# Two transformer blocks on one core: attention with its probabilities turned three steps after their scores in place of two

## The chip, the cores and the metric

The kernel runs on one core of a Trainium2 chip. The metric is the device time of one execution in microseconds (us), lower is better. Engines are named as in the profile: PE is TensorE's matmuls, PEld its weight loads, DVE is VectorE, ACT is ScalarE, POOL is GpSimd, SP is SyncE with the DMA queue.

## The reference, cut to what matters

Two blocks of two layers each work on 512 tokens of width 1024 in float32. Three of the four layers begin with an attention of 16 heads of 64, and these are what the change touches: a sparse one ("a" in the kernel), one with a forget gate ("b") and one with grouped keys over all tokens ("c"). All three have this core, for blocks of 128 queries:

```python
def one_block(q_blk):
    s = jnp.einsum('bqkgd,bskd->bkgqs', q_blk, k).astype(jnp.float32) * scale
    p = jax.nn.softmax(s, axis=-1).astype(v.dtype)
    return jnp.einsum('bkgqs,bskd->bqkgd', p, v)
```

In "a" a mask of selected keys is added to the logits, in "b" a decay and a causal mask. A block of queries i (0 to 3) in "a" and "b" needs only the first (i + 1) x 128 keys; in "c" it needs all 512. The rest of the model, projections and MLPs, is matmul work that the change leaves alone.

## The kernel before, in words

Every engine has its own program, in order, tied to the others by semaphores. Nothing is planned by a scheduler: the order is written out by hand, and each engine waits where its program says `wait_ge`.

One attention is `attend`, once in each of the programs of TensorE, ScalarE and VectorE. It goes through 32 steps (`STEPS`): 8 pairs of heads c, and for each the 4 query blocks i. A step has two rows (r = 2n and 2n + 1), one for each head of the pair. The life of step n:

- TensorE, `scores(n)`: two score matmuls (L525) into two of four banks; in "b" two more with the decay (L533). They wait until VectorE has emptied these banks of step n - 2.
- VectorE (L1254 in "a" and "b", L1252 in "c"): scales or masks the scores into the row's buffer `PROBS[a][r % 6]` (tiles PA, PBB, PC) and takes their extreme value. It waits until the buffer's old row has been turned.
- ScalarE (L917): the exponential in place, with its sum.
- VectorE (L1267, L1269), one iteration later: reciprocal of the sum, and the probabilities scaled by it.
- TensorE, `turn(n)` (L547), two iterations after the scores: transposes of 128x128 blocks into bank 4 (first row of the step) and bank 5 (second row). It waits for the scaled probabilities (`pn_done`) and for the copies that emptied these banks of step n - 1.
- The turned rows are copied into `TURNED` (tiles TA, TB, TC, six buffers each): the first row of the even steps by VectorE (L1261), all others by ScalarE (L926).
- TensorE, `values(n)` (L560), three iterations after the scores: the sums with the values into bank 6 or 7, by pair of heads.
- When the four steps of a pair are done, ScalarE copies its bank to `Xhi` (L930), and VectorE then takes the rest into `Xlo` (L1273). Both are at the ends of their iteration's part: iterations 7, 11, 15 and so on.

In an iteration n TensorE does scores(n), turn(n - 2), values(n - 3). VectorE does the scores of n, in even iterations the copy of step n - 2, the probabilities of step n - 1, and at 7, 11, ... the Xlo. ScalarE does the exponentials of n, its copies of step n - 2, and at 7, 11, ... the Xhi. In "a" VectorE also finishes the selection of keys (L1373, L1375) within its first three iterations. GpSimd makes the masks MH for "b" (L1691), one per pair of heads. The attention is followed by its output projection (L415 to L417), which reads Xhi and Xlo.

Of the kernel before, what the change touches and what calls it, by code (L numbers as in the profile page):

```python
# [9 lines left out]
F32 = mybir.dt.float32  # L10
F32R = mybir.dt.float32r

P = 128
# [5 lines left out]
EPS = 1e-6  # L19
BIG = 1e30  # L20
# [88 lines left out]
def body(nc, ctx, t, consts, out):  # L109
# [25 lines left out]
    stat = sb("stats", [P, 6, 4])  # L135
# [30 lines left out]
    with ExitStack() as region:  # L166
        QA = sb("QA", [P, KC, S], F32, region)
        KA = [sb(f"KA{i}", [P, S], F32, region) for i in range(4)]
        VA = sb("VA", [P, NT, 256], F32, region)
        PA = [sb(f"PA{i}", [P, S], F32, region) for i in range(6)]  # L170
        TA = [sb(f"TA{i}", [P, S], F32, region) for i in range(6)]
        QI, KI, WI = sb("QI", [P, 4, S], F32, region), sb("KI", [P, S], F32, region), sb("WI", [P, NT, 8], F32, region)
        SC = [sb(f"SC{i}", [P, S], F32, region) for i in range(3)]
        SC2, top = sb("SCW", [P, S], F32, region), sb("top", [P, 8], F32, region)
        RL = [sb(f"RL{i}", [P, S], F32, region) for i in range(3)]
        M = [sb(f"MA{i}", [P, (i + 1) * P], F32, region) for i in range(NT)]
        rope_a = sb("rope_a", [P, 2, S], F32, region)
# [6 lines left out]
    with ExitStack() as region:  # L184
        QB, KB, VB = sb("QB", [P, KC, S], F32, region), sb("KB", [P, KC, S], F32, region), sb("VB", [P, NT, D], F32, region)
        PBB = [sb(f"PBB{i}", [P, S], F32, region) for i in range(6)]
        TB = [sb(f"TB{i}", [P, S], F32, region) for i in range(6)]
        LF, FT = sb("LF", [P, 4, NT * 16], F32, region), sb("FT", [16, S], F32, region)
        CK, CQ = sb("CK", [P, S], F32, region), sb("CQ", [P, S], F32, region)
        MH = [sb(f"MH{i}", [P, S], F32, region) for i in range(2)]  # L190
        tsum, tri = sb("tsum", [P, S], F32, region), sb("tri", [P, S], F32, region)
    with ExitStack() as region:
        QC = sb("QC", [P, KC, S], F32, region)
        KCC = [sb(f"KC{i}", [P, S], F32, region) for i in range(4)]
        VC = sb("VC", [P, NT, 256], F32, region)
        PC = [sb(f"PC{i}", [P, S], F32, region) for i in range(6)]
# [166 lines left out]
    def tensor_program(pe):  # L363
# [151 lines left out]
        def attend(a, heads_q, heads_k, heads_v):  # L515
# [20 lines left out]
            def turn(n):  # L536
                for e in range(2):
                    r = 2 * n + e
                    pe_until.wait_ge(pn_done, base + r + 1)
                    if r >= 2:  # L540
                        by_act, by_dve = turned_by(a, r - 2)
                        if (r - 2) % 4:
                            pe_until.wait_ge(tr_act, by_act)
                        else:
                            pe_until.wait_ge(tr_dve, by_dve)
                    for j in range(0, width(a, STEPS[n][1]), P):
                        m = pe.transpose(bank[4 + e][:, j:j + P], PROBS[a][r % 6][:, j:j + P], ident[:])  # L547
                    m.then_inc(tr_full, 1)
# [281 lines left out]
    def scalar_program(act):  # L830
# [78 lines left out]
        def attend(a):  # L909
            base = 64 * ATT[a]  # L910
            for n in range(len(STEPS) + 4):
                if n < len(STEPS):
                    w = width(a, STEPS[n][1])
                    for r in (2 * n, 2 * n + 1):
                        p, st = PROBS[a][r % 6], stat[:, r % 6, :]
                        act_until.wait_ge(sc_out, base + r + 1)
                        act.activation(p[:, 0:w], p[:, 0:w], ACT_F.Exp, bias=st[:, 0:1], scale=-1.0, accum_out=st[:, 1:2]).then_inc(ex_done, 1)  # L917
                if 2 <= n < len(STEPS) + 2:
                    w = width(a, STEPS[n - 2][1])
                    for e in range(2):  # L920
                        r = 2 * (n - 2) + e
# [219 lines left out]
    def vector_program(dve):  # L1141
# [93 lines left out]
        def attend(a, mask, before=None):  # L1235
            base, hi0 = 64 * ATT[a], fill_base(a + "o")[0]
            for n in range(len(STEPS) + 4):
                if n < len(STEPS):
# [4 lines left out]
                    for r in (2 * n, 2 * n + 1):  # L1243
                        p, st = PROBS[a][r % 6], stat[:, r % 6, :]
# [10 lines left out]
                if 2 <= n < len(STEPS) + 2 and (2 * (n - 2)) % 4 == 0:  # L1255
                    r = 2 * (n - 2)
                    w = width(a, STEPS[n - 2][1])
# [4 lines left out]
                if 1 <= n < len(STEPS) + 1:  # L1262
                    w = width(a, STEPS[n - 1][1])
                    for r in (2 * n - 2, 2 * n - 1):
                        p, st = PROBS[a][r % 6], stat[:, r % 6, :]
# [4 lines left out]
                if n >= 4 and (n - 4) % NT == NT - 1:  # L1270
                    c = (n - 4) // NT
# [566 lines left out]
```

## Time and profile before

| | us |
|---|---|
| median of 3 runs | 2792.96 (2792.11 to 2793.75) |
| the profiled execution | 2792.17 |
| its span in the profile | 2790.6 |
| attention "a", first scores to the projection's first matmul | 110.61 |
| attention "b", the same | 99.95 |
| attention "c", the same | 111.55 |

Over the whole span PE is busy 2677.3 us (96%), its weight loads 2124.1, DVE 1331.2, ACT 968.6, POOL 1063.6. The three attentions lie at 155, 838 and 1456 us. In the timeline an entry begins with its start and its length in us; "x4" says how many instructions are merged into it; what stands in brackets is how long the engine had been idle before, and who released it. The first row of a step and the second have two instructions each in the scores, as a float32 matmul is recorded as two.

### The profile page before, as it was taken

What the parts mean: (1) busy time and instruction counts of PE and PEld (TensorE: products, weight loads), DVE (VectorE), ACT (ScalarE), POOL (GpSimd) and SP (SyncE); (2) the same over time, 40 slices, a digit from 0 to 9 for tenths busy, and PEclk for the clock granted to TensorE, in tenths of its full rate; (3) what the DMA queues carried; (4) which work ended last, traced back from release to release, by engine and by line L of the source; (5) the groups of instructions that cost most, each with busy time, mean ns of one, the idle gap of its engine ahead of it and who ended that gap; (6) DMA issues with size and microseconds to landing.
All of it is one profiled execution on the core that took longest, in us unless ns stands there. A gap on an engine that the chain in (4) does not pass through costs nothing.

```text
span 2790.6 us, 32354 instructions
## 1 busy us (share of the span) xinstructions
PE 2677.3 (96%) x13002; PEld 2124.1 (76%) x13002; DVE 1331.2 (48%) x2341; ACT 968.6 (35%) x1587; POOL 1063.6 (38%) x474
## 2 busy tenths in 40 slices
PE   8968999999998999999999999999999999999999
PEld 6645788887775678888775778888787888788887
DVE  4786598862016478883458542221325233332221
ACT  4345332222336432322437443322323232342231
POOL 4510444443451244444340234444444334344442
PEclk9979999999999999999999999999999999999999
DMA  4100455542220155553210123223332222233322
GB/s 138 61 16 16 128 186 183 186 139 76 92 91 1 46 160 191 183 184 98 83 61 1 46 77 105 91 92 104 123 105 69 91 91 77 76 105 97 99 91 76
DMA packets 259432, 274.42 MB, mean 98 GB/s; under 512 B 6868, under 2 KB 249300, under 8 KB 259028
## 3 DMA queue, kind: packets, MB, share of 16 engines
q1 hardware_dynamic: 259284, 272.37, 30.4%
q8 instruction: 103, 1.69, 0.3%
q14 instruction: 45, 0.37, 0.0%
HBM read 270.25 MB, written 2.10 MB: 98 GB/s over the span
## 4 chain that ended last, share of the span: by engine, by line
PE 90%; DVE 6%; ACT 3%; issue 1%; DMA 0%; POOL 0%; SPq 0%; DVEq 0%; ACTq 0%
PE bank L415 23%; PE bank L417 23%; PE bank L416 23%; PE bank L547 2%; PE bank L464 2%; PE bank L466 2%; PE bank L465 2%; PE bank L560 2%; PE bank L393 2%; PE bank L525 2%; PE bank L394 2%; PE bank L395 2%; DVE top L1373 1%; PE bank L795 1%; PE bank L513 1%
## 5 line engine op out<-in xcount | busy, mean ns | idle before, releaser
L1625 POOL TENSOR_TENSOR wlo<-raw,whi 128x1024 fp32r<-128x1024 f32 (+1 forms) x408 | 986.0, 2438 | 1504.2 <-ACT whi L844 1504.1
L415 PE MATMUL bank<-Xhi,whi 128*128 128x512 f32 (+1 forms) x1616 | 642.7, 398 | 7.0 <-POOL wlo L1625 6.9
L417 PE MATMUL bank<-Xhi,wlo 128*128 128x512 f32 (+1 forms) x1616 | 631.2, 391 | 0.0
L416 PE MATMUL bank<-Xlo,whi 128*128 128x512 f32 (+1 forms) x1616 | 630.7, 390 | 0.0
L844 ACT ACTIVATE whi<-raw 128x1024 fp32r<-128x1024 f32 (+1 forms) x408 | 404.9, 1041 | 591.3 <-PE bank L417 514.5
L415 PE MATMUL bank<-Hhi,whi 128*128 128x512 f32 x1024 | 406.7, 397 | 0.0
L416 PE MATMUL bank<-Hlo,whi 128*128 128x512 f32 x1024 | 404.9, 395 | 0.0
L417 PE MATMUL bank<-Hhi,wlo 128*128 128x512 f32 x1024 | 404.9, 395 | 0.0
L415 PEld LDWEIGHTS bank<-Xhi,whi 128*128 128x128 f32 (+1 forms) x1616 | 303.5, 188 | 78.3 <-issue 15.3
L416 PEld LDWEIGHTS bank<-Xlo,whi 128*128 128x128 f32 (+1 forms) x1616 | 303.6, 188 | 66.2 <-issue 3.6
L417 PEld LDWEIGHTS bank<-Xhi,wlo 128*128 128x128 f32 (+1 forms) x1616 | 303.2, 188 | 65.5
L1286 DVE SCALAR_TENSOR_TENSOR acc<-ada,cond,acc 128x256 f32<-128x256 f32 x336 | 345.8, 1029 | 12.0
L1190 DVE SCALAR_TENSOR_TENSOR HT<-bank,MOD,HT 128x512 f32<-128x512 f32 x96 | 72.0, 751 | 420.3 <-PE bank L417 401.3
L1319 DVE TENSOR_TENSOR tmp<-tmp 128x512 f32<-128x512 f32 x128 | 111.4, 871 | 258.0 <-ACT tmp L942 257.9
L417 PEld LDWEIGHTS bank<-Hhi,wlo 128*128 128x128 f32 x1024 | 192.4, 188 | 46.5
L416 PEld LDWEIGHTS bank<-Hlo,whi 128*128 128x128 f32 x1024 | 192.5, 188 | 45.5
L415 PEld LDWEIGHTS bank<-Hhi,whi 128*128 128x128 f32 x1024 | 192.4, 188 | 45.4
L942 ACT ACTIVATE tmp<-bank 128x512 f32<-128x512 f32 x128 | 76.5, 598 | 423.3 <-PE bank L417 408.4
L1188 DVE TENSOR_TENSOR HT<-bank,HT 128x512 f32<-128x512 f32 x80 | 55.1, 688 | 196.1 <-PE bank L417 196.1
L464 PE MATMUL bank<-whi,Xhi 128*128 128x512 f32 x256 | 101.9, 398 | 2.5 <-DVE Xlo L1167 2.5
L466 PE MATMUL bank<-whi,Xlo 128*128 128x512 f32 x256 | 100.4, 392 | 0.0
L465 PE MATMUL bank<-wlo,Xhi 128*128 128x512 f32 x256 | 100.4, 392 | 0.0
(257 smaller groups left out, 3000.1 us busy)
## 6 DMA issues: line engine op xcount, KB each, us to landing
ada<-in_ada_w SPq DMA_DIRECT2D x48, 1024.0 KB, 6.1
raw<-in_w_up SPq DMA_DIRECT2D x32, 1024.0 KB, 5.6
raw<-in_w_down SPq DMA_DIRECT2D x32, 1024.0 KB, 5.1
raw<-in_mlp_w_in SPq DMA_DIRECT2D x32, 1024.0 KB, 5.5
raw<-in_mlp_w_out SPq DMA_DIRECT2D x32, 1024.0 KB, 5.0
raw<-in_gmlp_w_in SPq DMA_DIRECT2D x24, 1024.0 KB, 5.1
raw<-in_gmlp_w_out SPq DMA_DIRECT2D x12, 1024.0 KB, 5.0
raw<-in_w_in_a SPq DMA_DIRECT2D x8, 1024.0 KB, 5.5
```

The source lines that it names most:

```text
L415: pe.matmul(b[0:rows, :], whi[s][:, c, j:j + rows], hi[:, c, :], start=(c == 0), stop=False)
L416: pe.matmul(b[0:rows, :], whi[s][:, c, j:j + rows], lo[:, c, :], start=False, stop=False)
L417: m = pe.matmul(b[0:rows, :], wlo[s][:, c, j:j + rows], hi[:, c, :], start=False, stop=(c == KC - 1))
L464: pe.matmul(b[:], Xhi[:, c, q * P:(q + 1) * P], hi[:, k, :], start=(c == 0), stop=False)
L465: pe.matmul(b[:], Xhi[:, c, q * P:(q + 1) * P], lo[:, k, :], start=False, stop=False)
L466: m = pe.matmul(b[:], Xlo[:, c, q * P:(q + 1) * P], hi[:, k, :], start=False, stop=(c == KC - 1))
L844: act.activation(whi[u % 2][:, c0:c1, 0:k], src[:, c0:c1, 0:k], ACT_F.Copy).then_inc(hi_done, 1)
L942: act.activation(tmp[v % 2][:], bank[(gm.tile + o) % 4][:], ACT_F.Relu).then_inc(up_q, 1)
L1190: dve.scalar_tensor_tensor(HT[:, o, :], b[:], gate[:, o:o + 1], HT[:, o, :], ALU.mult, ALU.add).then_inc(h_set, 1)
L1286: dve.scalar_tensor_tensor(a[:], src[:, c, :], cd[:, c:c + 1], a[:], ALU.mult, ALU.add).then_inc(ada_step, 1)
L1319: dve.tensor_tensor(r[:], tmp[v % 2][:], tmp[v % 2][:], ALU.mult).then_inc(up_r, 1)
L1625: pool.tensor_tensor(wlo[u % 2][:, c0:c1, 0:k], src[:, c0:c1, 0:k], whi[u % 2][:, c0:c1, 0:k].bitcast(F32), ALU.subtract).then_inc(lo_done, 1)
```

## The change

The distances and the number of row buffers get names. Rows are kept in 8 buffers in place of 6, with 8 places for their sums and extremes; the turn of a step follows its scores at three iterations in place of two, and its values at five in place of three. TensorE's order in an iteration becomes scores(n), turn(n - 3), values(n - 5). ScalarE and VectorE follow with their copies, and Xhi and Xlo come at iterations 9, 13, ... in place of 7, 11, ... The six buffers of turned rows stay, and so does who copies which row.

```diff
+ROWS, TURN, SUM = 8, 3, 5
...
-    stat = sb("stats", [P, 6, 4])
+    stat = sb("stats", [P, ROWS, 4])
...
-        PA = [sb(f"PA{i}", [P, S], F32, region) for i in range(6)]
+        PA = [sb(f"PA{i}", [P, S], F32, region) for i in range(ROWS)]
...
-                        m = pe.transpose(bank[4 + e][:, j:j + P], PROBS[a][r % 6][:, j:j + P], ident[:])
+                        m = pe.transpose(bank[4 + e][:, j:j + P], PROBS[a][r % ROWS][:, j:j + P], ident[:])
...
-            for n in range(len(STEPS) + 3):
+            for n in range(len(STEPS) + SUM):
                 if n < len(STEPS):
                     scores(n)
-                if 2 <= n < len(STEPS) + 2:
-                    turn(n - 2)
-                if n >= 3:
-                    values(n - 3)
+                if TURN <= n < len(STEPS) + TURN:
+                    turn(n - TURN)
+                if n >= SUM:
+                    values(n - SUM)
...
-                if n >= 4 and (n - 4) % NT == NT - 1:
-                    c = (n - 4) // NT
-                    act_until.wait_ge(pv_done, 32 * ATT[a] + n - 3)
+                if n > SUM and (n - SUM) % NT == 0:
+                    c = (n - SUM) // NT - 1
+                    act_until.wait_ge(pv_done, 32 * ATT[a] + n - SUM)
                     act.activation(Xhi[:, c, :], bank[6 + c % 2][:], ACT_F.Copy).then_inc(x_hi, 1)
...
-                        if r >= 6:
-                            dve_until.wait_ge(tr_full, base + r - 5)
+                        if r >= ROWS:
+                            dve_until.wait_ge(tr_full, base + r - ROWS + 1)
...
-                if 2 <= n < len(STEPS) + 2 and (2 * (n - 2)) % 4 == 0:
-                    r = 2 * (n - 2)
-                    w = width(a, STEPS[n - 2][1])
+                if TURN <= n < len(STEPS) + TURN and (n - TURN) % 2 == 0:
+                    r = 2 * (n - TURN)
+                    w = width(a, STEPS[n - TURN][1])
```

## Rows read from the trace of the kernel before

**Rows 1.** Busy time in the three attentions: PE, PEld, DVE, ACT, POOL; clock; DMA
```profile
155.06:265.67 110.61, 79.55 (x609) 49.02 (x609) 84.40 (x316) 58.41 (x183) 0.00 (x0) 0.84 0.01 1
838.13:938.08 99.95, 87.31 (x737) 54.74 (x737) 67.67 (x279) 59.56 (x184) 9.38 (x6) 1.00 0.00 1
1456.33:1567.88 111.55, 102.54 (x896) 64.48 (x897) 94.54 (x279) 76.52 (x184) 0.00 (x0) 1.00 0.01 1
```
**Rows 2.** By line: what L547 and L1273 waited for (us in all, times)
```profile
  DVE PC L1269: 42.2, 50
  DVE PA L1269: 42.0, 41
...
  ACT Xhi L930: 33.0, 24
```
**Rows 3.** Timeline of PE in "c": a period, and steps without a stall
```profile
1497.72 1.25 PE L547 MATMUL bank<-ident,PC 128*128 128x128 f32 x8 [0.89 <-DVE PC L1269]
...
1505.25 1.09 PE L560 MATMUL bank<-TC,VC 128*64 128x128 f32 x16
1506.28 1.13 PE L525 MATMUL bank<-KC,QC 64*128 64x512 f32 x4
...
1509.38 1.13 PE L525 MATMUL bank<-KC,QC 64*128 64x512 f32 x4
1511.40 1.25 PE L547 MATMUL bank<-ident,PC 128*128 128x128 f32 x8 [0.89 <-DVE PC L1269]
```
**Rows 4.** Timeline of VectorE and ScalarE in "c", around one Xlo
```profile
1502.43 0.69 DVE L1261 COPY TC<-bank 128x512 f32<-128x512 f32 x1
...
1504.33 0.75 DVE L1252 TENSOR_SCALAR_CACHE_REDUCE PC<-bank,RQ 128x512 f32<-128x512 f32 x1
...
1506.55 1.06 ACT L926 ACTIVATE TC<-bank 128x512 f32<-128x512 f32 x2
...
1507.50 0.59 ACT L930 ACTIVATE Xhi<-bank 128x512 fp32r<-128x512 f32 x1
1508.12 0.69 DVE L1273 TENSOR_TENSOR Xlo<-bank,Xhi 128x512 fp32r<-128x512 f32 x1 [1.18 <-ACT Xhi L930]
...
1508.73 0.74 DVE L1252 TENSOR_SCALAR_CACHE_REDUCE PC<-bank,RQ 128x512 f32<-128x512 f32 x1
```
**Rows 5.** Timeline of "a": PE's stalled turns, VectorE and ScalarE between them
```profile
202.82 0.84 PE L547 MATMUL bank<-ident,PA 128*128 128x128 f32 x6 [1.32 <-ACT TA L926]
...
206.14 0.42 DVE L1254 CUSTOM_DVE_ANT_0 PA<-bank,MA 128x256 f32<-128x256 f32 x1
...
207.60 1.06 ACT L926 ACTIVATE TA<-bank 128x512 f32<-128x512 f32 x2
...
208.62 0.56 DVE L1254 CUSTOM_DVE_ANT_0 PA<-bank,MA 128x384 f32<-128x384 f32 x1 [0.92 <-PE bank L525]
...
210.44 0.25 ACT L926 ACTIVATE TA<-bank 128x128 f32<-128x128 f32 x1
...
213.89 0.84 PE L547 MATMUL bank<-ident,PA 128*128 128x128 f32 x6 [1.32 <-ACT TA L926]
...
214.53 0.69 DVE L1273 TENSOR_TENSOR Xlo<-bank,Xhi 128x512 fp32r<-128x512 f32 x1 [0.94 <-ACT Xhi L930]
...
215.55 0.55 DVE L1261 COPY TA<-bank 128x384 f32<-128x384 f32 x1
```
**Rows 6.** Timeline of PE in "b": two stalled turns, a period apart
```profile
858.11 0.84 PE L547 MATMUL bank<-ident,PBB 128*128 128x128 f32 x6 [1.09 <-ACT TB L926]
...
870.53 0.85 PE L547 MATMUL bank<-ident,PBB 128*128 128x128 f32 x6 [1.09 <-ACT TB L926]
```
**Rows 7.** The ends of "a" and "b" on PE, and a stretch's busy time with its clock
```profile
262.48 3.26 PE L560 MATMUL bank<-TA,VA 128*64 128x128 f32 x28
...
936.30 1.85 PE L560 MATMUL bank<-TB,VB 128*64 128x128 f32 x28
...
262.00:264.00 2.00, 2.00 (x17) 1.67 (x17) 0.00 (x0) 0.93 (x2) 0.00 (x0) 0.50 0.00 0
```

More of the change, by code:

```diff
@@ L185, in body @@
         QB, KB, VB = sb("QB", [P, KC, S], F32, region), sb("KB", [P, KC, S], F32, region), sb("VB", [P, NT, D], F32, region)
-        PBB = [sb(f"PBB{i}", [P, S], F32, region) for i in range(6)]
+        PBB = [sb(f"PBB{i}", [P, S], F32, region) for i in range(ROWS)]
         TB = [sb(f"TB{i}", [P, S], F32, region) for i in range(6)]
@@ L195, in body @@
         VC = sb("VC", [P, NT, 256], F32, region)
-        PC = [sb(f"PC{i}", [P, S], F32, region) for i in range(6)]
+        PC = [sb(f"PC{i}", [P, S], F32, region) for i in range(ROWS)]
         TC = [sb(f"TC{i}", [P, S], F32, region) for i in range(6)]
@@ L910, in attend @@
             base = 64 * ATT[a]
-            for n in range(len(STEPS) + 4):
+            for n in range(len(STEPS) + SUM + 1):
                 if n < len(STEPS):
@@ L914, in attend @@
                     for r in (2 * n, 2 * n + 1):
-                        p, st = PROBS[a][r % 6], stat[:, r % 6, :]
+                        p, st = PROBS[a][r % ROWS], stat[:, r % ROWS, :]
                         act_until.wait_ge(sc_out, base + r + 1)
                         act.activation(p[:, 0:w], p[:, 0:w], ACT_F.Exp, bias=st[:, 0:1], scale=-1.0, accum_out=st[:, 1:2]).then_inc(ex_done, 1)
-                if 2 <= n < len(STEPS) + 2:
-                    w = width(a, STEPS[n - 2][1])
+                if TURN <= n < len(STEPS) + TURN:
+                    w = width(a, STEPS[n - TURN][1])
                     for e in range(2):
-                        r = 2 * (n - 2) + e
+                        r = 2 * (n - TURN) + e
                         if r % 4:
@@ L1236, in attend @@
             base, hi0 = 64 * ATT[a], fill_base(a + "o")[0]
-            for n in range(len(STEPS) + 4):
+            for n in range(len(STEPS) + SUM + 1):
                 if n < len(STEPS):
@@ L1243, in attend @@
                     for r in (2 * n, 2 * n + 1):
-                        p, st = PROBS[a][r % 6], stat[:, r % 6, :]
+                        p, st = PROBS[a][r % ROWS], stat[:, r % ROWS, :]
                         b = bank[2 * (n % 2) + r % 2]
                         dve_until.wait_ge(sc_full, base + r + 1)
-                        if r >= 6:
-                            dve_until.wait_ge(tr_full, base + r - 5)
+                        if r >= ROWS:
+                            dve_until.wait_ge(tr_full, base + r - ROWS + 1)
                         mk = mask(i, w)
@@ L1254, in attend @@
                             dve.tensor_tensor_reduce(p[:, 0:w], b[:, 0:w], mk, -0.125, 3e38, ALU.add, ALU.min, st[:, 0:1]).then_inc(sc_out, 1)
-                if 2 <= n < len(STEPS) + 2 and (2 * (n - 2)) % 4 == 0:
-                    r = 2 * (n - 2)
-                    w = width(a, STEPS[n - 2][1])
+                if TURN <= n < len(STEPS) + TURN and (n - TURN) % 2 == 0:
+                    r = 2 * (n - TURN)
+                    w = width(a, STEPS[n - TURN][1])
                     dve_until.wait_ge(tr_full, base + r + 1)
@@ L1264, in attend @@
                     for r in (2 * n - 2, 2 * n - 1):
-                        p, st = PROBS[a][r % 6], stat[:, r % 6, :]
+                        p, st = PROBS[a][r % ROWS], stat[:, r % ROWS, :]
                         dve_until.wait_ge(ex_done, base + r + 1)
@@ L1269, in attend @@
                         dve.tensor_scalar(p[:, 0:w], p[:, 0:w], st[:, 2:3], None, ALU.mult).then_inc(pn_done, 1)
-                if n >= 4 and (n - 4) % NT == NT - 1:
-                    c = (n - 4) // NT
+                if n > SUM and (n - SUM) % NT == 0:
+                    c = (n - SUM) // NT - 1
                     dve_until.wait_ge(x_hi, hi0 + c + 1)
```

## The prediction

> **What bounds the kernel now.** I read the three attentions first as stretches, since the change touches nothing else. They last 110.61, 99.95 and 111.55 us, together 322.1 of a span of 2790.6 us, and in none of them is an engine full: PE records 79.55, 87.31 and 102.54 us, DVE 84.40, 67.67 and 94.54, ACT less [rows 1]. Then I read who is waited for. The transposes (L547) have waits of 42.0 us on the scaled probabilities (L1269) in "a" and 42.2 in "c", PE's and the weight loads' own records counted together; and VectorE sat idle for 33.0 us ahead of its 24 instructions on L1273, waiting for ScalarE's Xhi (L930) [rows 2]. The first wait is what the change names. The second lies in VectorE's queue, ahead of the next step's scores (L1252, L1254).
>
> Last I read single steps. In "c" a step without a stall takes PE 3.10 us (1506.28 to 1509.38), a period of four 13.68 (from one stalled turn at 1497.72 to the next at 1511.40), so 13.68 - 4 x 3.11 = 1.25 us of every period are idle [rows 3]. They come from one place. In every fourth iteration, which I call the flush, VectorE ends its probabilities at 1506.94, waits 1.18 us for Xhi, runs L1273 (0.61 us to the next issue) and takes the next scores at 1508.73 [rows 4]; those were ready about 1507.4, and all that follows is late. The period of "a" is 11.07 us (202.82 to 213.89); PE's first stall in it is 1.32 us, on ScalarE's pair of copies (L926), and the rest is on L1269 [rows 5]. That of "b" is 12.42, with 1.09 on ScalarE's copies [rows 6].
>
> **PE without stalls.** By the steps that don't wait, scores take PE 1.06 us at 512 columns and 0.21 less per 128 columns, a transposed pair 0.37, 0.58, 0.78 or 1.02 us by width, the values 0.37, 0.58, 0.81 or 1.03 (1505.25 to 1506.28) [rows 3]. Summed over the widths 128 to 512: "a" 8.5 us a period, "b" about 10.7 (its masks add matmuls), "c" 12.43. VectorE's own sums with L1273 are 8.5 in "a" and "b" and 12.4 in "c". So there are 2.5, 1.7 and 1.25 us a period to win, and in "a" and "c" PE and VectorE would then be tied.
>
> **The change, part by part.**
> (1) Turning at three steps. The wait on L1269 goes: it is ready a whole iteration ahead. Next late is the copy out of the transposes' bank, since the transposes of iteration n wait for the copies of iteration n-1, which stand on ScalarE behind that iteration's two exponentials. This tie does not get looser by the change.
> (2) The parity. VectorE copies the even steps' first row (L1261). With distance 2 that fell in even iterations, with distance 3 in odd ones; the flush, with values at five in place of three, falls at 9, 13, ... in place of 7, 11, ..., odd both times. So VectorE's copy now lies in the flush iteration, where ScalarE has one copy ahead of Xhi in place of two. In "c", counted from VectorE's start of the scores: ScalarE's copies start at +2.22 (1504.33 to 1506.55), one copy is 0.48, Xhi 0.59, so Xhi is there at +3.3; VectorE, 1.34 for two scores and 1.90 for copy and probabilities (1502.43 to 1504.33), comes at +3.22 [rows 4]. The wait of 1.18 falls to 0.1. In "a" and "b" the flush moves from the 512 wide step to the 256 wide one: Xhi at 1.46 + 0.37 + 0.59 = +2.42, VectorE, with two scores and the scaled probabilities in 1.49 (206.14 to 208.62, less 0.92 idle and 0.07 that overlap) and the copy in 0.47, at +1.96 [rows 5]; the wait goes from 0.94 to 0.45.
> (3) The new stall. The flush iteration now holds copy and L1273 on VectorE. "c": 3.32 + 0.61 = 3.93 us against PE's 3.11, so VectorE starts the next scores 0.82 late, and that iteration is the one where ScalarE copies both rows; the first is there 2.22 + 0.58 + 0.11 = 2.91 after VectorE's start, PE wants it at 3.00 less the lag, which stalls it 0.73. Period 12.43 + 0.76 = 13.2, gain 0.49. "a": VectorE takes 2.42 + 0.03 + 0.61 = 3.06 where PE takes 1.78; the lag is 1.07, and ScalarE's pair of 512 columns (1.06 us for both, from +1.82) has its first row at +2.52 [rows 5]; PE's transposes wait 1.03 and for the second row another 0.37: period 9.9, gain 1.15. "b": PE is slower by its mask matmuls and the lag is gone before it counts. Its stall of 1.09 on a 256 wide pair becomes one on a single 128 wide copy: 0.11 shorter, PE comes 0.23 later (that iteration now has 128 transposed and 384 of values in place of 256 and 128), and only the second row waits, 0.21 later still: 0.54. Period 11.25, gain 1.17.
> (4) Values at five. No wait is removed by it, since the turn has already waited for later copies; it costs nothing in the stream and sets the parity of (2).
> (5) Eight rows. The scores of step n wait for the turn of step n-4, in PE's iteration n-1, as they did with six rows and distance 2. Nothing, in time; below nothing too, as no transfer and no engine's work hangs on it.
> (6) Start. Before the ninth scores "a" and "b" have paid one flush now and none after; against it, PE waits for the first copies, one iteration later than now. Followed from the first scores with the durations above, the ninth scores start earlier by 1.2 in "a" (between 0.5 and 2.5, for whose mean clock of 0.84 [rows 1] means some 35 us at the lower of the two levels, 1.2 GHz, nearly all of them in its first 30 us), 2.2 in "b", 0.4 in "c".
> (7) End. Behind the last scores PE has one more turn and two more values to do: 2.0 us in "a" and "b", 3.1 in "c", against the stalls that they fill. From the scores of step 29 to the end I get -0.4 in "b", +0.6 in "c", -0.7 in "a". In "a" the granted clock is 0.50 there; its last 28 value matmuls took 3.26 us where those of "b" took 1.85 [rows 7]. With the turn before them that is 2.1 us. PE idles before that fall, and the added distance puts work in this idle time, so I take the 2.1 as gained (bounds 0 and 2.1).
>
> Queues passed: SP and GpSimd have nothing in an attention that moves against PE, but for the masks of "b", which are made well ahead (they wait on scores three steps earlier). What follows waits for the last Xlo only in its eighth chunk, behind some 4.8 us of matmuls, so an attention ends with PE's last values.
>
> **Sum.** Five periods lie between scores 9 and 29. "a": 1.2 + 5 x 1.15 + 0.7 + 2.1 = 9.8. "b": 2.2 + 5 x 1.17 + 0.4 = 8.5. "c": 0.4 + 5 x 0.49 - 0.6 = 2.25. Together 20.5 us. The profiled execution took 2792.17 us (1.6 outside the span) and would take 2771.7; the median of the runs is 0.8 above it, which gives 2772.5.
>
> **A rule against it.** VectorE's occupancy in "a" and "c" is above that of the weight loads (84.40 against 49.02 us, 94.54 against 64.48) [rows 1], and the change takes no work from it. The Trainium skill, "Perfetto Trace Analysis", section "Identifying the Most-Contended Engine", says to improve the engine with the highest occupancy, and to judge TensorE by its weight loads. By it VectorE is the bound and "a" and "c" gain nothing; only the 8.5 of "b" would stay and the time would be 2784. The trace speaks against it: VectorE stands idle 26 us in "a" and 17 in "c" [rows 1], and it idles for the others' order, not for work.
>
> **Rivals.**
> A. *Xhi's wait stays at its present length*, because ScalarE runs late in the flush. For it: 33.0 us over 24 instructions, at each one [rows 2]. Against: one copy less ahead of it. "c": 3.22 + 1.17 + 0.61 = 5.0, lag 1.9, period 14.2, slower than now; "a" loses half of its gain, "b" almost nothing. In all about 13 us: 2780.
> B. *No new stall*: ScalarE's copies come in time. PE's own sums then stand: another 5 x (1.4 + 0.55 + 0.75) = 13.5 us: 2759. Against it: ScalarE already makes PE wait 1.32 and 1.09 us [rows 5, 6].
> C. *The stall only changes its name* (the other side). If the copies in ScalarE's queue, not the probabilities, set the pace everywhere, periods stay as they are and each attention pays for its two more iterations: 2.0 + 2.0 + 3.1 = 7.1 us behind the last scores: 2800. It decides from the point where the new stall reaches the old idle time, 2.5 us a period in "a", 1.7 in "b", 1.25 in "c"; I have 1.4, 0.55 and 0.75. "c" is nearest to it.
> D. *VectorE is the bound*: "a" and "c" keep their periods, since its queue is as full as before, and only the 8.5 of "b" stays: 2784. If PE never was held by L1269 either: 2793. For it: 85% of "c". Against: the 17 us idle.
>
> **How the numbers follow.** Forecast 0.72, A 0.11, B 0.04, C 0.06, D 0.07 (about half of it within 0.2% of now). The range of 2764 to 2784 takes the unknowns of the start and the clock (3 us either way), half of B and all of A. A measurement of this kernel can tell about 0.2%, 5.6 us. Faster 0.89, the same 0.05, slower 0.06.
>
> **What would show it.** Right: waits of L547 on L1269 nearly gone but for starts and ends; L1273's wait on Xhi below 15 us in all; L547's waits on L926 up, to some 20 us; periods near 9.9, 11.25 and 13.2; the clock at 1.0 to the end of "a". Wrong: L1273 still waiting a microsecond each time (A); PE waiting on L1252 or L1254 for its scores (D); periods unchanged (C).

## The result and the profile after

| | before | after |
|---|---|---|
| median, us | 2792.53 (2791.62 to 2793.75, 4 runs) | 2752.41 (2750.61 to 2754.87, 4 runs) |
| span of the profiled execution, us | 2790.6 | 2749.3 |
| attention "a" | 110.61 | 99.05 |
| attention "b" | 99.95 | 92.81 |
| attention "c" | 111.55 | 108.97 |

The ratio of after to before is 0.9857, with a 95% interval of 0.9844 to 0.987. That is 40 us where 20.5 had been forecast, and below the range. Line numbers of after are two higher than those of before: L549 is the turn, L562 the values, L928 ScalarE's copies, L932 Xhi, L1275 Xlo.

The three attentions, again as stretches (the columns are those of [rows 1]: length, then PE, PEld, DVE, ACT and POOL busy, granted clock, DMA):

```profile
155.01:254.06 99.05, 75.44 (x608) 46.55 (x608) 84.38 (x316) 57.92 (x183) 0.00 (x0) 0.86 0.01 1
820.79:913.60 92.81, 87.95 (x736) 56.14 (x736) 67.48 (x279) 59.58 (x184) 9.52 (x6) 0.98 0.01 1
1427.03:1536.00 108.97, 101.23 (x897) 65.22 (x897) 94.46 (x279) 76.57 (x184) 0.00 (x0) 1.00 0.01 2
```

They are shorter by 11.56, 7.14 and 2.58 us, together 21.3. So the attentions did what was forecast (20.5), and the other 20 us of the 41.3 by which the span fell lie where nothing was changed. The starts show it too: "b" begins 17.3 us earlier though "a" gained 11.6, "c" 29.3 earlier though "a" and "b" gained 18.7. A view of the groups by line finds them. First before, then after (busy us in all, mean ns of one):

```profile
L415 PE MATMUL bank<-Xhi,whi 128*128 128x512 f32 (+1 forms) x1616 | 642.7, 398 | 7.0 <-POOL wlo L1625 6.9
L415 PE MATMUL bank<-Hhi,whi 128*128 128x512 f32 x1024 | 406.7, 397 | 0.0
L416 PE MATMUL bank<-Hlo,whi 128*128 128x512 f32 x1024 | 404.9, 395 | 0.0
L417 PE MATMUL bank<-Hhi,wlo 128*128 128x512 f32 x1024 | 404.9, 395 | 0.0
```
```profile
L417 PE MATMUL bank<-Xhi,whi 128*128 128x512 f32 (+1 forms) x1616 | 642.5, 398 | 8.1 <-POOL wlo L1627 8.1
L417 PE MATMUL bank<-Hhi,whi 128*128 128x512 f32 x1024 | 400.5, 391 | 0.0
L419 PE MATMUL bank<-Hhi,wlo 128*128 128x512 f32 x1024 | 398.8, 389 | 0.0
L418 PE MATMUL bank<-Hlo,whi 128*128 128x512 f32 x1024 | 398.3, 389 | 0.0
```

The same 3072 matmuls of the MLPs' second half, which read Hhi and Hlo (buffers of type float32r), cost 18.9 us less (1216.5 to 1197.6), some 6 ns each, while those on Xhi kept their time. Nothing in them was edited. What did change for them is where Hhi lies: `stats` grew from 96 to 128 bytes per partition, and all buffers allocated behind it start 32 bytes higher.

Now the attentions' single steps, read as in [rows 3 to 6]. "c" on all three engines:

```profile
1486.49 1.11 PE L549 MATMUL bank<-ident,PC 128*128 128x128 f32 x8 [0.67 <-ACT TC L928]
...
1495.04 0.57 ACT L928 ACTIVATE TC<-bank 128x512 f32<-128x512 f32 x1
1495.52 0.58 ACT L932 ACTIVATE Xhi<-bank 128x512 fp32r<-128x512 f32 x1
1495.56 0.49 DVE L1271 TENSOR_SCALAR PC<-PC,stats 128x512 f32<-128x512 f32 x1
...
1496.14 0.69 DVE L1275 TENSOR_TENSOR Xlo<-bank,Xhi 128x512 fp32r<-128x512 f32 x1
...
1499.68 1.11 PE L549 MATMUL bank<-ident,PC 128*128 128x128 f32 x8 [0.67 <-ACT TC L928]
```

The period is 13.19 us (1486.49 to 1499.68). Xlo's wait is down from 1.18 to 0.09 us, since only one copy stands ahead of Xhi: VectorE ends its probabilities at 1496.05, and Xlo starts at 1496.14, just behind the end of Xhi (so short a wait is printed by no view here). The new stall of PE is 0.67 us, on a copy of the iteration where ScalarE makes both. "a":

```profile
203.65 0.69 DVE L1275 TENSOR_TENSOR Xlo<-bank,Xhi 128x512 fp32r<-128x512 f32 x1 [0.42 <-ACT Xhi L932]
...
206.78 0.30 PE L549 MATMUL bank<-ident,PA 128*128 128x128 f32 x1 [0.92 <-ACT TA L928]
...
207.26 0.30 PE L549 MATMUL bank<-ident,PA 128*128 128x128 f32 x1 [0.18 <-ACT TA L928]
...
216.65 0.30 PE L549 MATMUL bank<-ident,PA 128*128 128x128 f32 x1 [0.92 <-ACT TA L928]
```

A period of 9.87 us, Xlo's wait 0.42, the new stall 0.92 and 0.18. "b", two turns a period apart, and the ScalarE copy just ahead of the second:

```profile
851.39 0.41 PE L549 MATMUL bank<-ident,PBB 128*128 128x128 f32 x2 [0.40 <-DVE PBB L1271]
...
862.29 0.26 ACT L928 ACTIVATE TB<-bank 128x128 f32<-128x128 f32 x1
862.69 0.41 PE L549 MATMUL bank<-ident,PBB 128*128 128x128 f32 x2 [0.40 <-DVE PBB L1271]
```

11.30 us, with a stall of 0.40 on a second row. The row names L1271, but the scaled probabilities that this turn reads were made an iteration earlier; the copy out of its bank ended at 862.55, and that is what it needed (it starts 0.14 us later, as the stalled turn of "c" at 1499.68 starts 0.14 behind the end of its copy). Such a name is inferred from which engine signalled last, and here that signal was not the one waited for. The end of "a", as a stretch:

```profile
251.94:254.06 2.12, 2.12 (x37) 1.94 (x36) 0.34 (x1) 0.76 (x2) 0.00 (x0) 1.00 0.04 8
```

The granted clock is 1.00 to the last value, where it had been 0.50 [rows 7]. Last, the idle time ahead of Xlo, from the view of line 1275, which was 33.0 for all 24 [rows 2]:

```profile
  ACT Xhi L932: 16.2, 18
```

Of these 16.2 us, 11.1 are the last two Xlo of each attention, where VectorE has little else left to do.

### The profile page after: what moved, and what is told of

Same layout as the page of the kernel before. It is cut to its first block, busy times and chain, and to the rows that moved or that the text cites. A ratio compares the mean times of both kernels' runs of the same rounds, so it can differ in the third digit from the quotient of the medians.

```text
span 2749.3 us, 32372 instructions
## 1 busy us (share of the span) xinstructions
PE 2650.4 (96%) x13002; PEld 2119.3 (77%) x13002; DVE 1332.0 (48%) x2341; ACT 968.4 (35%) x1587; POOL 1063.4 (39%) x474
## 4 chain that ended last, share of the span: by engine, by line
PE 89%; DVE 6%; ACT 3%; issue 1%; POOL 1%; DMA 0%; SPq 0%; DVEq 0%; ACTq 0%; POOLq 0%
PE bank L417 23%; PE bank L419 23%; PE bank L418 23%; PE bank L549 2%; PE bank L466 2%; PE bank L467 2%; PE bank L468 2%; PE bank L562 2%; PE bank L527 2%; PE bank L395 1%; PE bank L396 1%; PE bank L397 1%; DVE top L1375 1%; PE bank L797 1%; ACT PC L919 1%
## 5 line engine op out<-in xcount | busy, mean ns | idle before, releaser
L417 PE MATMUL bank<-Xhi,whi 128*128 128x512 f32 (+1 forms) x1616 | 642.5, 398 | 8.1 <-POOL wlo L1627 8.1
L417 PE MATMUL bank<-Hhi,whi 128*128 128x512 f32 x1024 | 400.5, 391 | 0.0
L419 PE MATMUL bank<-Hhi,wlo 128*128 128x512 f32 x1024 | 398.8, 389 | 0.0
L418 PE MATMUL bank<-Hlo,whi 128*128 128x512 f32 x1024 | 398.3, 389 | 0.0
L417 PEld LDWEIGHTS bank<-Xhi,whi 128*128 128x128 f32 (+1 forms) x1616 | 303.3, 188 | 79.4 <-issue 16.0
L417 PEld LDWEIGHTS bank<-Hhi,whi 128*128 128x128 f32 x1024 | 192.3, 188 | 39.4
```

The lines of the kernel that those rows point to most:

```text
L417: pe.matmul(b[0:rows, :], whi[s][:, c, j:j + rows], hi[:, c, :], start=(c == 0), stop=False)
L418: pe.matmul(b[0:rows, :], whi[s][:, c, j:j + rows], lo[:, c, :], start=False, stop=False)
L419: m = pe.matmul(b[0:rows, :], wlo[s][:, c, j:j + rows], hi[:, c, :], start=False, stop=(c == KC - 1))
```

## The experiments

Two questions stood. Where do the 20 us outside the attentions come from? And which part of the change carries the attentions' gain: the distance of turning, the distance of the values, the rows, or the parity of the flush? A pair like (2, 4) says how many iterations behind its scores a step is turned and has its values; before is (2, 3), after (3, 5). Each ratio is to the kernel before, run beside it. "Distance" below, where it is of places, is the byte address of the streamed operand (Xhi, Hhi, Yhi and their lo parts) in its partition, less that of the weight buffer.

**The place, with the old order.**

```diff
-    stat = sb("stats", [P, 6, 4])
+    stat = sb("stats", [P, 8, 4])
```

> The kernel before, with one edit: stats, a buffer of 96 bytes per partition, is made 128 bytes long. No instruction changes; every buffer that is allocated behind it (XT, QA, PA, Hhi, Hlo, QB, QC, VT, Yhi) starts 32 bytes higher: at byte 124032 of its partition in place of 124000, a multiple of 64 where it was none. Theory 1 (the 20 us outside the attentions come from where Hhi and Hlo start): the float32r matmuls of 512 columns that read Hhi and Hlo fall from 397/395/395 ns to about 391/389/389, those that read Xhi and Xlo stay at 398/391/390, the kernel takes 2772 to 2774 us, and the three attentions keep about their 110.6, 100.0 and 111.5 us. Theory 2 (the 20 us are a consequence of the new order or of the two more rows): no difference, 2792 to 2794 us.

Measured: 2775.58 us, ratio 0.9943 (0.9928 to 0.9957).

```profile
L415 PE MATMUL bank<-Hhi,whi 128*128 128x512 f32 x1024 | 400.5, 391 | 0.0
L417 PE MATMUL bank<-Hhi,wlo 128*128 128x512 f32 x1024 | 398.8, 389 | 0.0
L416 PE MATMUL bank<-Hlo,whi 128*128 128x512 f32 x1024 | 398.3, 389 | 0.0
```

These are after's rows to a tenth of a microsecond, in a kernel that has before's order. Its periods are 11.06, 12.43 and 13.69 us, as before. Theory 1 holds, if 1.6 us above its band; 32 more bytes in the buffer of the row statistics are worth 17 us. The four stretches outside the attentions (155.1, 572.5, 518.3 and 1222.7 us before) are 155.0, 566.8, 512.0 and 1215.7, 19.0 less; in after 155.0, 566.7, 513.4 and 1213.3, 20.0 less.

**The order, with the old place**: `stat` of the kernel after made `[P, 14, 4]`.

> The kernel after, with stats made 224 bytes long in place of 128, so that the buffers behind it start at byte 124128: 96 bytes past a multiple of 128, as in the kernel before. Order, distances and the eight rows stay. Theory 1 (place): the matmuls on Hhi and Hlo are back at 397/395/395 ns and only the attentions' gain is left, 2771 to 2774 us. Theory 2 (order or rows): still 2752 us.

Measured: 2775.98 us, ratio 0.9944 (0.9929 to 0.9959); Hhi and Hlo at 395, 396 and 396 ns. The attentions of its profile take 98.76, 94.39 and 108.94 us, 302.1 together, 20.0 less than before. The whole is 2 us over the expected band, and the profiled execution, at 2779.16 us, is 5. In its profile 3.5 us lie ahead of the first attention and 4.6 in the matmuls on Xhi and Xlo, which ran at 399, 391 and 391 ns; the first attention of other kernels here began up to 2.3 us earlier and 4.3 later than before's, so I take it as scatter. By its stretches, what the forecast priced was worth what it was priced at.

Taken singly by the medians, the place gives 17 us and the order 16, together 33 of the 40. The mean granted clocks of the four profiles are 0.978 (before), 0.977, 0.977 and 0.980 (after), and 0.001 of the clock over this span is 2.8 us (an estimate that lets all of the time go with the clock). So most of the other 7 us may be the clock, which was higher in after than in either single change; that is not shown.

**How far must it be moved?** The kernel before with `stats` of 160 and of 192 bytes.

> The kernel before with stats made 160 bytes long: the buffers behind it start at byte 124064, 32 past a multiple of 64 as before, but 32 in place of 96 past one of 128. If a multiple of 64 is what counts, the matmuls on Hhi stay at 397/395/395 ns and the time at 2793 us; if the price is that of a row of 2048 bytes that starts 96 bytes into a stretch of 128, another value between 389 and 400 ns is to be expected. By theory 2 2793 us.

Measured: 2793.56 us, ratio 1.0007 (0.9997 to 1.0016), 397/395/395 ns on Hhi and Hlo: nothing gained, as its first alternative had it.

> The kernel before with stats made 192 bytes long: the buffers behind it start at byte 124096, a multiple of 64 and not of 128. If a multiple of 64 is enough, 391/389/389 ns on Hhi and Hlo and 2772 to 2774 us, as with 128 bytes; if 128 is what counts, 397/395/395 ns and 2793 us. By theory 2 2793 us.

Measured: 2778.77 us, ratio 0.9956 (0.9941 to 0.9971).

```profile
L415 PE MATMUL bank<-Hhi,whi 128*128 128x512 f32 x1024 | 404.0, 394 | 0.0
L417 PE MATMUL bank<-Hhi,wlo 128*128 128x512 f32 x1024 | 400.7, 391 | 0.0
L416 PE MATMUL bank<-Hlo,whi 128*128 128x512 f32 x1024 | 399.6, 390 | 0.0
...
L415 PE MATMUL bank<-Yhi,whi 128*128 128x512 f32 x144 | 56.4, 392 | 0.0
```

Neither alternative fits: a multiple of 64 gives most of the gain on Hhi, not all of it. And Yhi, which lies elsewhere, is at its best here (392 against 399 before and 397 in after).

**Is it the streamed operand's own place?** An unused buffer of 32 bytes ahead of raw, whi and wlo; then the same ahead of Xhi.

```diff
+    sb("pad", [P, 8])
     raw = [sb(f"raw{i}", [P, KC, UC]) for i in range(2)]
```

> The kernel before with an unused buffer of 32 bytes put ahead of raw and the weight buffers whi and wlo. These now start 32 bytes past a multiple of 64 (whi0 at byte 67744), and the buffers of the regions (Hhi, Hlo and the rest) at 124032, a multiple of 128. Theory 1 (the start of the operand that streams through a matmul counts, that of the loaded weights does not): Hhi and Hlo at 391/389/389 ns; the weight loads stay at 188 ns; the 4848 matmuls on Xhi and Xlo with whi and wlo as loaded weights stay at 398/391/390; the 768 of the lines 464 to 466, in which whi and wlo stream, go from 398/392/392 up by some 6 ns. 2777 to 2783 us. If the start of whatever is read counts, weights too, the gain on Hhi is lost again and the time is 2790 us or more.

Measured: 2830.1 us, ratio 1.0133 (1.0118 to 1.0148).

```profile
L416 PE MATMUL bank<-Xhi,whi 128*128 128x512 f32 x1600 | 645.9, 404 | 6.6 <-POOL wlo L1626 6.5
...
L416 PE MATMUL bank<-Hhi,whi 128*128 128x512 f32 x1024 | 406.6, 397 | 0.0
```

> The kernel before with an unused buffer of 32 bytes put ahead of Xhi and Xlo: these and everything up to the regions start 32 bytes past a multiple of 64 (Xhi at byte 18592), the regions at 124032. Theory 1: the 4848 matmuls on Xhi and Xlo (lines 415 to 417) rise by about 6.3 ns each, 30 us, the 768 in which whi and wlo stream and the 384 of lines 393 to 395 by some 7 us, Hhi and Hlo fall to 391/389/389: slower than the kernel before although Hhi is well placed, 2805 to 2816 us. If the place counts only for Hhi and Hlo, for some reason of their own, 2775 to 2780 us.

Measured: 2793.69 us, ratio 1.0000 (0.9991 to 1.0009).

```profile
L416 PE MATMUL bank<-Xhi,whi 128*128 128x512 f32 x1600 | 636.5, 398 | 8.2 <-POOL wlo L1626 8.2
...
L416 PE MATMUL bank<-Hhi,whi 128*128 128x512 f32 x1024 | 406.7, 397 | 0.0
```

In both the theory that the streamed operand's own place counts fell; of the alternatives, the first one's (the gain on Hhi is lost again) came true, the second one's did not. Together they give the answer. With only the weights moved, Xhi has become slow without having been moved. With Xhi and the weights moved together, Xhi is fast at an address 32 bytes past a multiple of 128, and Hhi at a multiple of 128 is slow. So it isn't the address of the streamed operand that counts but its distance from the weights.

**Does raw have a part, and how far does the distance count?** raw was moved along with the weights in the first of these two. In the next kernel raw is moved by 32 bytes and whi and wlo by 128; in the one after, raw by 32 and whi and wlo by 256. In both `stats` has 128 bytes as well, which keeps the distance of Hhi from whi at a multiple of 256.

> The kernel before with raw alone moved (the buffers into which the weights land from memory, and from which ScalarE and GpSimd make whi and wlo); whi, wlo, Xhi, Xlo, Hhi and Hlo at multiples of 128. If it is TensorE's own two reads that collide, nothing is lost: 391/389/389 ns on Hhi and Hlo, 2773 to 2778 us. If the place of raw, and with it ScalarE's or GpSimd's accesses beside TensorE's, was the cause in the run with raw, whi and wlo moved: 2790 us or more.

Measured: 2802.86 us, ratio 1.0032 (1.002 to 1.0043).

```profile
L417 PE MATMUL bank<-Xhi,whi 128*128 128x512 f32 x1600 | 642.6, 402 | 8.0 <-POOL wlo L1627 8.0
...
L417 PE MATMUL bank<-Hhi,whi 128*128 128x512 f32 x1024 | 400.6, 391 | 0.0
```

Read by its second alternative this would blame raw. But raw feeds the weights of both, and only Xhi is slower: it now lies 128 bytes off from whi, while Hhi's distance is still a multiple of 256.

> The kernel before with raw 32 bytes past a multiple of 128 and with whi and wlo 256 bytes further from Xhi than before; Hhi and Hlo at a distance from whi that is a multiple of 256. Theory (only the distance between the streamed operand and the weights counts, in bytes modulo 256): Xhi and Xlo at 398/391/390 ns and Hhi and Hlo at 391/389/389, Yhi at a distance of 192 stays at 397/394/394, 2773 to 2778 us. If raw's place counts: Xhi and Xlo at 402/395/395 as in the last run, 2790 us or more.

Measured: 2775.21 us, ratio 0.9926 (0.991 to 0.9943), Xhi at 398/391/391 ns and Hhi at 391/389/389. Raw has no part in it, and a shift of 256 bytes is no shift. All the runs give one table; the three numbers are the means in ns of the matmuls (hi, whi), (lo, whi) and (hi, wlo):

| distance modulo 256 | where | ns | loss |
|---|---|---|---|
| 0 | Hhi after; Yhi with `stats` of 192 | 391/389/389; 392/389/389 | 0 |
| 32 | Hhi with `stats` of 160 | 397/395/395 | 6 |
| 64 | Hhi with `stats` of 192 | 394/390/391 | 2 |
| 96 | Hhi, after misplaced | 395/396/396 | 6 |
| 128 | Xhi, weights moved by 128 | 402/395/395, at 0 398/391/390 | 4 |
| 160 | Yhi before | 399/396/397 | 7 |
| 192 | Yhi after | 397/394/394 | 5 |
| 224 | Hhi before; Xhi, weights moved by 32 | 397/395/395; 404/397/397 | 6 |

**Which of the three matmuls pays?** wlo alone moved by 32, then whi alone (32 bytes ahead of whi, 96 ahead of wlo, and `stats` of 128 bytes).

> The kernel before with an unused buffer of 32 bytes put ahead of the two wlo buffers: whi, Xhi, Xlo and Hhi, Hlo start at multiples of 128 bytes, wlo alone 32 past one. The stream of matmuls on a chunk is (whi, hi) in line 416, (whi, lo) in 417, (wlo, hi) in 418 (one line further than in the kernel before), and the weights of each are loaded during the one ahead of it. Theory P (a matmul pays if its own two operands are apart): line 418 rises by 6 ns, to 395 on Hhi and 397 on Xhi, 416 and 417 keep 391/389 and 398/391; 2792 us. Theory Q (a matmul pays if what it streams and the weights loaded meanwhile are apart): line 417 rises by 6 ns, to 395 on Hlo and 397 on Xlo, and 418 keeps 389 and 391; 2792 us as well. If only a pair with the whole set of weights apart pays: 2776 us.

Measured: 2822.48 us, ratio 1.0106 (1.009 to 1.0123).

```profile
L417 PE MATMUL bank<-Hlo,whi 128*128 128x512 f32 x1024 | 409.1, 400 | 0.0
L416 PE MATMUL bank<-Hhi,whi 128*128 128x512 f32 x1024 | 406.1, 397 | 0.0
L418 PE MATMUL bank<-Hhi,wlo 128*128 128x512 f32 x1024 | 398.6, 389 | 0.0
```

> The kernel before with whi alone moved: whi starts 32 bytes past a multiple of 128, raw, wlo, Xhi, Xlo, Hhi and Hlo at multiples of 128. Theory Q (charged to the matmul during which the moved weights are loaded): whi is loaded during line 416's matmul (for 417) and during line 418's (for the next 416), so these two rise and 417, during which wlo is loaded, keeps 389 on Hlo. Theory P (charged to the owner): 416 and 417 rise, 418 keeps 389; the run with wlo alone spoke against it. If moving one buffer costs 17 ns per three matmuls whichever it is, as wlo did: 2815 to 2825 us. If by 6 ns per load of moved weights: 12 per three, 2805 to 2812 us.

Measured: 2806.99 us, ratio 1.0044 (1.0028 to 1.0061); Hhi and Hlo at 396/393/393 ns with whi at a distance of 96 and wlo at 0, Xhi and Xlo at 404/393/393 with whi at 224 and wlo at 128. Theory P is refuted by the first: the one matmul that owns the moved wlo is the only one that pays nothing. Theory Q has its largest loss in the right place (11 ns on L417, during which wlo is loaded), but not its size, and does not explain the 6 on L416. The second refutes it too: the matmul during which wlo is loaded should have kept its 389 ns and took 393. Its time is in the band of "6 ns per load of moved weights", but by that rule wlo alone would cost 6 ns in three matmuls, and it cost 17. How the loss is shared stays open. Whose accesses collide can be narrowed by one more reading of the traces: on Hhi in the first MLP, three matmuls that ran wholly while neither GpSimd nor ScalarE's weight split was busy follow each other at 0.700 us before (109 of them) and 0.682 with `stats` of 128 bytes (106), the same 18 ns as on the average. So it is not the other engines' writing of whi and wlo. What is left, and fits all the runs, is that TensorE loses it on its own two kinds of reads; no trace shows the accesses themselves.

**The rows and the distances.** All with eight rows and the good place; only `TURN` and `SUM` differ.

> The kernel after with its distances put back to those of before: turned at two steps, values at three, and the eight rows kept (so stats has its 128 bytes, and the buffers behind it start at byte 124032). Theory 1 (the rows act through the place of the other buffers alone): as the kernel before with stats of 128 bytes, 2773 to 2778 us, periods of 11.07, 12.43 and 13.68 us per column of heads in the three attentions, waits of 0.94, 0.91 and 1.18 us ahead of VectorE's Xlo. Rival (a row that is free two steps earlier shortens the loop): periods below these and under 2770 us.

Measured: 2773.5 us, ratio 0.9926 (0.991 to 0.9943), with before's periods. The two more rows do nothing at (2, 3) but move the other buffers.

> Eight rows, turned at two steps as before, values at four. Theory 1 (the distance of turning carries the gain, since the transposes then find their rows normalised, the copies on ScalarE come early and Xhi behind them): the waits ahead of Xlo stay near 0.9 to 1.2 us, the transposes go on waiting for the normalised row, periods within 0.2 us of 11.07, 12.43 and 13.68, 2770 to 2778 us. Rival (the values' distance carries it, since the values then no longer wait for the copies): periods near 9.9, 11.3 and 13.2 and 2752 to 2758 us.

Measured: 2753.44 us, ratio 0.9852 (0.9838 to 0.9867). The time is the rival's, and so are the periods but for that of "a" (10.34).

> Eight rows, turned at three steps, values at four: one step between a copy and its values, as before, and the flush of a column now falls into an iteration in which ScalarE makes both copies. Theory 1 (distance of turning): most of the gain stays, yet Xhi stands behind two copies, so that the wait ahead of Xlo is longer than the 0.42, 0.42 and 0.0 us of the kernel after by up to one copy (about 0.6 us): periods of 9.9 to 10.5, 11.3 to 11.9 and 13.2 to 13.7, 2752 to 2766 us. Rival (values' distance): as in the kernel before with well-placed buffers, 2773 to 2778 us.

Measured: 2751.29 us, ratio 0.9852 (0.9836 to 0.9869); the periods are those of theory 1, but for 11.07 in "b", which is shorter, and the time is 0.7 us below its band.

**The flush spread over two iterations.** VectorE's Xlo moved to the next iteration, behind its score rows, with the distances of after.

```diff
+                if n > SUM + 1 and (n - SUM) % NT == 1:
+                    c = (n - SUM) // NT - 1
+                    dve_until.wait_ge(x_hi, hi0 + c + 1)
+                    dve.tensor_tensor(Xlo[:, c, :], bank[6 + c % 2][:], Xhi[:, c, :].bitcast(F32), ALU.subtract).then_inc(x_lo, 1)
                 if TURN <= n < len(STEPS) + TURN and (n - TURN) % 2 == 0:
...
-                if n > SUM and (n - SUM) % NT == 0:
```

> The kernel after with VectorE's Xlo subtraction moved from the end of the iteration in which ScalarE writes Xhi to the next one, behind that iteration's score rows. If the 0.69 us of Xlo and its wait of 0.42 us push the score rows, and with them the exponentials and the copies, back, moving them behind the rows gives back some 0.6 us per column in the first two attentions and up to 0.7 in the third: periods of 9.3, 10.9 and 12.5 us, 2740 to 2748 us. Rival (VectorE is the bound of the loop, so that an operation costs the same wherever it stands, and only its wait of 0.42 us goes): 9.5, 10.9 and 13.2 us, 2745 to 2750 us. Rival (another instruction waits in its place): 2752 us.

Measured: 2743.85 us, ratio 0.9821 (0.9806 to 0.9836). "a" and "c" did as expected; "b" kept its 11.29, since its PE is still held 0.40 us a period at the same turn.

> VectorE's Xlo one iteration later, as in the run with it, at the distances of two and four. With two and four the wait ahead of Xlo was zero already, in the flush iteration VectorE does its copy as well, and moving Xlo spreads these over two iterations: periods of 12.43 us in the third attention (PE's own sum), 9.7 to 10.1 in the first, 11.2 in the second, 2745 to 2750 us. If nothing is late any more in the third but PE itself, it can't fall under 12.43.

Measured: 2747.5 us, ratio 0.9835 (0.9818 to 0.9851), all as expected.

> VectorE's Xlo one iteration later, at the distances of three and four. The wait of Xlo for Xhi goes here too (0.57, 0.57 and 1.18 us in the run without the move), but Xlo now falls into an iteration with VectorE's copy, ahead of that copy: periods of 9.4 to 9.9, 11.06 and 12.7 to 13.2 us, 2743 to 2750 us. If only the wait counts and not what shares the iteration: 12.43 to 12.5 in the third attention and 2741 us.

Measured: 2745.17 us, ratio 0.9828 (0.9814 to 0.9843), as expected but for "a", 0.1 us below its band.

> Eight rows, Xlo one iteration later, and for each attention the distances that gave its shortest stretch in the runs: three and five in the first, three and four in the second, two and four in the third. If the attentions are independent of each other, their stretches are those seen with these distances, 96.2, 90.4 and 104.2 us, and the whole is 2.2 us less than with three and five throughout: 2739 to 2744 us. Periods of 9.35, 11.07 and 12.43 us.

Measured: 2742.27 us, ratio 0.9821 (0.9807 to 0.9836). Stretches of 96.76, 93.55 and 104.17 us; "b" has the expected period but a mean granted clock of 0.96, where the run with three and four had 1.00 and 90.44 us.

The periods are the differences of the starts of neighbouring Xlo in the timeline, with Xlo's wait in brackets; within a run they agree to 0.02 us:

| turned, values | Xlo | "a" | "b" | "c" |
|---|---|---|---|---|
| 2, 3 | as it was | 11.07 (0.94) | 12.43 (0.91) | 13.69 (1.18) |
| 2, 4 | as it was | 10.34 (0) | 11.20 (0) | 13.18 (0.09) |
| 3, 4 | as it was | 9.95 (0.57) | 11.07 (0.57) | 13.69 (1.18) |
| 3, 5 (after) | as it was | 9.87 (0.42) | 11.29 (0.42) | 13.18 (0.09) |
| 2, 4 | one later | 9.73 (0) | 11.18 (0) | 12.43 (0) |
| 3, 4 | one later | 9.30 (0) | 11.07 (0) | 13.00 (0) |
| 3, 5 | one later | 9.35 (0) | 11.29 (0) | 12.43 (0) |

Two rows show what the rest is made of. With two and four, then three and four, "c":

```profile
1459.29 0.58 ACT L932 ACTIVATE Xhi<-bank 128x512 fp32r<-128x512 f32 x1
1459.90 0.69 DVE L1275 TENSOR_TENSOR Xlo<-bank,Xhi 128x512 fp32r<-128x512 f32 x1
```
```profile
1466.64 0.69 DVE L1275 TENSOR_TENSOR Xlo<-bank,Xhi 128x512 fp32r<-128x512 f32 x1 [1.18 <-ACT Xhi L932]
```

In "c" only the parity counts. The flush falls beside VectorE's copy with (2, 4) and (3, 5), and beside two ScalarE copies with (2, 3) and (3, 4); the periods are 13.18 in the one pair and 13.69 in the other, whatever the distance of turning. The two pairs differ in one thing more: with (2, 4) and (3, 5) the values come two iterations behind the turn, with (2, 3) and (3, 4) one. That was the rival's cause for (2, 4), values that no longer wait for the copies. The traces speak against it: PE has no wait at its value matmuls in any of these kernels, before (L560) included. It waits at turns alone, and what differs ahead of them is VectorE's wait for Xhi, 1.18 against 0.09 us.

In "a" and "b" either way alone gives most of it: (2, 4), with the parity of after, 0.73 and 1.23 us a period; (3, 4), one more step of both distances, 1.12 and 1.36; (3, 5) 1.20 and 1.14. They fill the same idle time and do not add up. So my expectation for (2, 4), that nothing is gained while the turn stays at two, fell. It left out the parity, which the prediction had. And it took the wait on the scaled probabilities for a consequence of the short distance: with (2, 4) the turn is as near as before, yet in the periods of all three attentions PE waits on ScalarE's copies alone (1.39, 0.44 and 0.67 us). The probabilities had been late because the flush ahead of them was.

## Why the prediction was wrong, and where it was right

**The step that failed** is part (5): "Nothing, in time; below nothing too, as no transfer and no engine's work hangs on it". That reasoned about who waits for a row, and took the rest of the kernel as untouched. The missing term is 3072 matmuls by 6 ns, 18.9 us of busy time and 19 to 20 us of the stretches outside the attentions, on top of 20.5. With Hhi at a distance that costs as much as that of before (96 bytes modulo 256, in place of 224), after takes 2775.98 us, inside the range and 3.5 above the forecast. No rival had this case, for all of them were about the attentions.

**The sum** of the attentions, 20.5 against 21.3, is in part luck: its three terms were off by +1.8, -1.4 and +0.3 us.

**Part (1), the wait on L1269 goes**: right for PE itself, whose own waits on it were 9.2, 7.7 and 3.2 us in "a", "c" and "b" and are 0.6, none and 3.4 (these last are the misnamed ones). But the longer distance was not needed for it: (2, 4) keeps the turn at two, loses the wait as well and has most of the gain.

**Part (2), the parity**: shown, by the two pairs of "c" and their waits. Xlo's wait was forecast at 0.1 in "c" and 0.45 in "a" and "b"; it is 0.09 and 0.42. The sum over all is 16.2 us where "below 15" was said, as the ends of the attentions hold 11.1 of it.

**Part (3), the new stall**: forecast 0.73 in "c", 1.03 and 0.37 in "a", 0.54 in "b"; measured 0.67, 0.92 and 0.18, 0.40. (The lag of 1.07 us in "a" has no working: 3.06 less 1.78 is 1.28.) The periods of 9.9, 11.25 and 13.2 came out as 9.87, 11.29 and 13.18. Only the waits on ScalarE's copies were put too high, at some 20 us in all: they are 6.6 in "a" and 5.5 in "c", and others of 5.1 are on VectorE's.

**Part (4), the values at five**: it sets the parity, as said, and "c" needs it (13.69 with four, 13.18 with five); in "b" it costs 0.22 a period. In the whole, (3, 4) and (3, 5) can't be told apart: 2751.29 and 2752.41 us.

**Parts (6) and (7)**: "a" gained 11.56 where the sum had 9.8, "b" 7.14 where it had 8.5, "c" 2.58 where it had 2.25. The clock at the end of "a" did stay up, and not by chance: in all eleven profiles with (2, 3) it is at 0.50 for 3 to 7 us that begin in the last 8 of "a", in none of the eight with longer distances. Of "b" part is its clock, 1.00 in the trace of before and 0.98 in that of after; in nine other kernels with the old order and a mean clock of 0.97 or 0.98 it took 100.3 to 102.1 us.

**The rivals.** A (Xhi's wait stays) and C (the stall only changes its name) are refuted by the periods. B (no new stall) did not happen in after, but moving Xlo one iteration on made it happen: "c" then has 12.43 us, the sum of PE's own work in the prediction, and PE has no wait in these periods. D (VectorE is the bound) is refuted by the same runs: VectorE has the same instructions in all of them, and "a" went from 11.07 to 9.35 us. After shows VectorE busy for 84.38 of 99.05 us in "a", the fullest engine there. The Trainium skill, "Perfetto Trace Analysis", section "Identifying the Most-Contended Engine", would optimise it first, and as the prediction read that rule, "a" would have gained nothing. The traces don't bear this out: "a" gained 11.56 us with all of VectorE's work kept, and moving one of its instructions, with no work taken from it, gave another 2.8 us (99.05 to 96.21).

**Better than both**: eight rows, three and five, Xlo one iteration later, 2743.85 us; 8.6 us below after, with intervals of the ratios that don't overlap (0.9806 to 0.9836 against 0.9844 to 0.987). The kernel with its own distances in each attention, 2742.27 us, can't be told from it.

## What to carry to other kernels

A buffer that grows moves every buffer behind it. Before pricing an edit at nothing outside its own stretch, list what is allocated later and which matmuls read it; a one-line pad that restores the old places, and one that moves the places with the old order, separate the two causes at once. When a distance in a software pipeline is changed, work out for each side job in which iteration it falls and what else that engine does there: here that parity was all of the gain in one attention, and moving one 0.69 us instruction to the next iteration gave 8.6 us more, with no distance changed. And a wait that names a late result is not yet a reason to ask for that result later: here what made it late was another job ahead of it in the queue.

## What the runs showed of the hardware

A float32r matmul of 512 columns, one of a stream of them each with its own 128x128 weights, takes 4 to 7 ns longer when the streamed operand and the weight buffers don't lie at the same byte modulo 256 of their partitions (2 ns at 64); distances that are multiples of 32 were tried. It makes no difference which of the two is streamed: the matmuls that stream whi and wlo with Xhi and Xlo as weights went from 398/392/392 to 404/399/399 ns when whi and wlo moved by 32. Matmuls follow each other at about 227 ns at the best (0.682 us for three), so that is up to 3%, and 55 us of this kernel when it hits nearly all of its float32r matmuls (2830.1 against 2775.58 us). Of absolute alignment no effect was seen: Xhi and whi both 32 bytes past a multiple of 128 are as good as both on one (398/391/391 against 398/391/390 ns). The Trainium skill, "SBUF — State Buffer", section "Who interferes with whom", gives TensorE two read ports, one for the moving operand and one for the weight loads, and calls them independent. The traces here don't agree: what each matmul takes depends on where the one lies against the other, and the loss of 18 ns in three is there with GpSimd and ScalarE's weight split idle. The measurement decides; what the two ports share is not shown. Of the attentions' plain float32 matmuls little can be said. The operands of the scores and of the values all lie behind `stats` and move together, so their distances never changed; only those of the transposes did, and they kept a median of 273 ns in every kernel.
